# Five of the sixteen table slots read in the pause ahead of the qkv projection

## The reference, cut to what matters

```python
# first block, even layer: x += mixer; x += swiglu(rms_norm(x, e_ln_ffn), ...)   F = 2816
# first block, odd layer:
h = rms_norm(x, o_ln_mix)
q, k, v = split(h @ o_w_qkv)                 # 1024 x 3072; differential attention, 8 heads, causal
x = x + (attention(q, k, v) @ o_w_o)
x = x + moe(rms_norm(x, o_ln_ffn))           # 8 experts, top 2
# second block, layer l = 0, 1 (adaLN):
def adaln(cond, w, b):                       # w is 1024 x 6144
    m = jax.nn.silu(cond) @ w + b            # shift, scale, gate for the mixer and for the FFN
```

## Time and profile before

| | |
|---|---|
| median of 3 runs | 2750.06 us (2749.29 to 2752.14) |
| the profiled execution's own time | 2748.68 us |
| its span | 2746.9 us |
| mean granted TensorE clock | 0.992 |
| PE busy | 2642.2 us, 96% |
| DVE busy | 1903.7 us, 69% |
| ACT busy | 1400.0 us, 51% |
| DMA, mean over the span | 224 GB/s |

### The profile page before, as it was taken

The page is one execution under the profiler, slowest core; times in us unless marked ns, Lnnn a source line. Parts: engine busy times, 40 slices in busy tenths (PEclk is TensorE's granted clock), DMA queues, the critical chain, the costliest instruction groups (busy, mean ns, idle before and its releaser), DMA issues.

```text
span 2746.9 us, 46870 instructions
## 1 busy us (share of the span) xinstructions
PE 2642.2 (96%) x18575; PEld 2274.2 (83%) x18575; DVE 1903.7 (69%) x2824; ACT 1400.0 (51%) x2246; POOL 0.2 (0%) x4
## 2 busy tenths in 40 slices
PE   8899999988999999999999999999999999999998
PEld 7575997846989898989898989964899999865897
DVE  3765555746888888888888888675655655664654
ACT  2411333343777677777776777363443443253432
POOL 0000000000000000000000000000000000000000
PEclk9999999998999999999999999999999999999999
DMA  6535552584888898889898989020645442221551
GB/s 259 230 115 232 201 187 88 186 350 172 330 338 331 335 335 329 339 326 343 326 343 324 341 322 353 35 93 1 249 178 188 176 181 111 102 113 70 186 185 58
DMA packets 57000, 615.07 MB, mean 224 GB/s; under 512 B 6448, under 2 KB 6704, under 8 KB 6704
## 3 DMA queue, kind: packets, MB, share of 16 engines
q1 hardware_dynamic: 56448, 610.20, 58.8%
q10 hardware_dynamic: 432, 3.15, 0.3%
HBM read 612.28 MB, written 1.05 MB: 223 GB/s over the span
## 4 chain that ended last, share of the span: by engine, by line
PE 83%; DVE 11%; ACT 3%; issue 2%; DMA 1%; DVEq 0%; SPq 0%; ACTq 0%
PE psum L1611 8%; PE psum L1613 8%; PE psum L1612 7%; PE psum L320 6%; PE psum L322 6%; PE psum L321 6%; PE psum L510 5%; PE psum L1638 4%; PE psum L1640 4%; PE psum L1639 4%; PE psum L335 3%; PE psum L336 3%; PE psum L337 3%; PE psum L661 2%; PE psum L1996 1%
## 5 line engine op out<-in xcount | busy, mean ns | idle before, releaser
L404 DVE TENSOR_TENSOR r_high<-ring,r_high 128x1024 fp32r<-128x1024 f32 x936 | 1089.9, 1220 | 115.5 <-ACT r_high L366 114.3
L366 ACT ACTIVATE r_high<-ring 128x1024 fp32r<-128x1024 f32 x624 | 626.3, 1060 | 6.3 <-DMA ring<-stream_dram 6.3
L1611 PE MATMUL psum<-r_high 128*128 128x256 f32 x1792 | 513.8, 287 | 15.7 <-DVE r_high L1823 15.6
L1613 PE MATMUL psum<-r_high 128*128 128x256 f32 x1792 | 507.9, 283 | 0.0
L1612 PE MATMUL psum<-r_high 128*128 128x256 f32 x1792 | 507.6, 283 | 0.0
L320 PE MATMUL psum<-r_low,r_high 128*128 128x256 f32 x1408 | 399.8, 284 | 1.8 <-DVE r_high L480 1.8
L322 PE MATMUL psum<-r_low,r_high 128*128 128x256 f32 x1408 | 398.4, 283 | 0.0
L1611 PEld LDWEIGHTS psum<-r_high 128*128 128x128 f32 x1792 | 342.6, 191 | 44.3 <-issue 27.9
L1612 PEld LDWEIGHTS psum<-r_high 128*128 128x128 f32 x1792 | 342.8, 191 | 5.9 <-issue 1.7
L1613 PEld LDWEIGHTS psum<-r_high 128*128 128x128 f32 x1792 | 343.1, 191 | 0.0
L370 ACT ACTIVATE r_high<-ring 128x1024 fp32r<-128x1024 f32 x312 | 329.6, 1056 | 0.0
(11 more groups left out here) (494 smaller groups left out, 4189.7 us busy)
## 6 DMA issues: line engine op xcount, KB each, us to landing
ring<-stream_dram SPq DMA_DIRECT2D x384, 1536.0 KB, 8.1
arena<-bias_dram ACTq DMA_DIRECT2D x2, 1024.0 KB, 7.8
pack<-pack_dram SPq DMA_DIRECT2D x1, 1664.0 KB, 17.3
const<-const_dram SPq DMA_DIRECT2D x1, 1124.0 KB, 13.8
x<-x_dram SPq DMA_DIRECT2D x1, 1024.0 KB, 5.1
xc<-ctx_dram SPq DMA_DIRECT2D x1, 1024.0 KB, 24.9
arena<-band_dram ACTq DMA_DIRECT2D x1, 1024.0 KB, 5.2
out_dram<-x SPq DMA_DIRECT2D x1, 1024.0 KB, 3.9
```

The lines of the kernel that those rows point to most:

```text
L366: act.activation(w_hi[:, i % 2, part * D:part * D + D], slot_of[r][:, part * D:part * D + D], ACT.Copy)\
L404: ins = dve.tensor_tensor(lo, slot_of[r][:, o:o + D], hi.bitcast(f32), SUB)
L1611: pe.matmul(dst, xe_hi[:, k, :], hi, start=(k == 0), stop=False)
L1613: ins = pe.matmul(dst, xe_lo[:, k, :], hi, start=False, stop=(k == KD - 1))
```

## The change

The second table is read in two parts. Five of its slots (`ADA_EARLY`) stand in the ring ahead of the qkv slots: four are read right behind the FFN, in place of six of nine idle products, and the fifth behind the transposes of the norm, in place of three of five. The other eleven follow the qkv slots: eight in units 0 to 7 of the attention and three behind the loop, as before. In the ring the order is now ada1 49 to 53, qkv 54 to 61, ada1 62 to 72. In DRAM all of `ada1` stands ahead of `qkv`, and SP's loop, written out from slot 48 to 75, maps one to the other (`DRAM_AT`, `RING_AT`). `ada_z_dve(dve, 1)` moves from behind the qkv columns to just ahead of `ffn_dve`, and its array and that of the copied rows move into constants no longer used (`g2`, `w2a2`). The first part is copied out of PSUM by ACT between `x_hi` and the sine, and DVE adds the second part from PSUM behind the scaling by the root. The remaining idle products write bank 5, since bank 7 now holds the table.

```diff
 STREAM = [
...
-    ("qkv", QKV // COLS), ("ada1", ADA_SLOTS), ("o_out", 3),
+    ("ada1", ADA_SLOTS), ("qkv", QKV // COLS), ("o_out", 3),
...
+ADA_EARLY = 5
+RING_AT = {_name: FIRST[_name] for _name in FIRST}
+RING_AT["qkv"] = FIRST["ada1"] + ADA_EARLY
+RING_AT["ada1_rest"] = RING_AT["qkv"] + QKV // COLS
+DRAM_AT = [*range(FIRST["ada1"], FIRST["ada1"] + ADA_EARLY), *range(FIRST["qkv"], FIRST["o_out"]),
+           *range(FIRST["ada1"] + ADA_EARLY, FIRST["qkv"])]
...
-        cond_z = [ar(o, KD * 62, "p (k n) -> p k n", k=KD) for o in (29200, 25600)]
-        ada_rows = [ar(o, COLS) for o in (28816, 27648)]
+        cond_z = [t.rearrange("p (k n) -> p k n", k=KD) for t in (ar(29200, KD * 62), mat("g2")[:, 0:KD * 62])]
+        ada_rows = [ar(28816, COLS), mat("w2a2")[:, 0:COLS]]
...
         def ada_slot(l, s):
+            if l:
+                return RING_AT["ada1"] + s if s < ADA_EARLY else RING_AT["ada1_rest"] + s - ADA_EARLY
...
-            starts = (0,) if l else (0, ADA_SPLIT)
+            starts = (0, ADA_EARLY if l else ADA_SPLIT)
...
-        def ada_rows_dve(dve):
+        def ada_rows_dve(dve, l):
 
-            slot_used(dve, ada_slot(0, ADA_SLOTS - 1))
-            dve.wait_ge(sem("ada_rows"), 1)
-            step(dve, dve.tensor_tensor(ada_rows[0], ada_rows[0], psum[:, 6, 0:COLS], ADD), "ada_rows")
+            slot_used(dve, ada_slot(l, ADA_SLOTS - 1))
+            dve.wait_ge(sem("ada_rows"), 2 * l + 1)
+            step(dve, dve.tensor_tensor(ada_rows[l], ada_rows[l], psum[:, 6 + l, 0:COLS], ADD), "ada_rows")
...
             diff_cols_dve(dve)
-            ada_z_dve(dve, 1)
...
                 S(dve.tensor_tensor(v, v, rstd[:, 8 * j:8 * j + 8].unsqueeze(2).to_broadcast([P, 8, P]), MUL), "df_on")
+            ada_rows_dve(dve, 1)
...
                 act.activation(x_hi[:, half, :], hT[:, half, 0:T], ACT.Copy).then_inc(sem("px_hi"), 1)
+            ada_rows_act(act, 1, ADA_EARLY)
             diff_cols_act(act)
...
             root_act(act, 16)
-            ada_rows_act(act, 1)
...
-                if n < ADA_1:
-                    ada_pe(pe, 1, n, n + 1)
+                if ADA_EARLY + n < ADA_1:
+                    ada_pe(pe, 1, ADA_EARLY + n, ADA_EARLY + n + 1)
...
-            with sp.Fori(1, min(G_MOE, g_end)) as g:
+            n0, n1 = FIRST["ada1"], FIRST["o_out"]
+            with sp.Fori(1, n0 // RING) as g:
                 for r in range(RING):
                     sp.wait_ge(w_used[r], g)
                     sp.dma_start(slot_of[r], stream_in[g * RING + r]).then_inc(w_ready[r], 16)
+            for n in range(n0 // RING * RING, G_MOE * RING):
+                sp.wait_ge(w_used[n % RING], n // RING)
+                sp.dma_start(slot_of[n % RING], stream_in[DRAM_AT[n - n0] if n0 <= n < n1 else n])\
+                  .then_inc(w_ready[n % RING], 16)
...
             ffn_pe(pe, 0, "e_ffn")
-            idle_pe(pe, 9)
+            ada_pe(pe, 1, 0, ADA_EARLY - 1)
+            idle_pe(pe, 3, 5)
             norm_pe(pe, 2)
-            idle_pe(pe, 5)
+            ada_pe(pe, 1, ADA_EARLY - 1, ADA_EARLY)
+            idle_pe(pe, 2, 5)
             diff_pe(pe)
...
             ada_mods_dve(dve, 0)
+            ada_z_dve(dve, 1)
             ffn_dve(dve, 0, "e_ffn")
```

More of the change, by code:

```diff
@@ L571, in ada_slot @@
         def ada_slot(l, s):
+            if l:
+                return RING_AT["ada1"] + s if s < ADA_EARLY else RING_AT["ada1_rest"] + s - ADA_EARLY
             late = s - (ADA_SLOTS - ADA_LATE)
-            return FIRST["ada0_late"] + late if l == 0 and late >= 0 else FIRST[f"ada{l}"] + s
+            return FIRST["ada0_late"] + late if late >= 0 else FIRST["ada0"] + s
         def ada_pe(pe, l, s0, s1):
@@ L590, in ada_pe, with ada_rows_act @@
                 ins.then_inc(w_used[n % RING], 1)
-        def ada_rows_act(act, l, slots=ADA_SLOTS):
+        def ada_rows_act(act, l, slots):
             slot_used(act, ada_slot(l, slots - 1))
             act.activation(ada_rows[l], psum[:, 6 + l, 0:COLS], ACT.Copy).then_inc(sem("ada_rows"), 1)
-        def ada_rows_dve(dve):
-            slot_used(dve, ada_slot(0, ADA_SLOTS - 1))
-            dve.wait_ge(sem("ada_rows"), 1)
-            step(dve, dve.tensor_tensor(ada_rows[0], ada_rows[0], psum[:, 6, 0:COLS], ADD), "ada_rows")
+        def ada_rows_dve(dve, l):
+            slot_used(dve, ada_slot(l, ADA_SLOTS - 1))
+            dve.wait_ge(sem("ada_rows"), 2 * l + 1)
+            step(dve, dve.tensor_tensor(ada_rows[l], ada_rows[l], psum[:, 6 + l, 0:COLS], ADD), "ada_rows")
         def ada_tr_pe(pe, l):
-            pe.wait_ge(sem("ada_rows"), l + 2)
+            pe.wait_ge(sem("ada_rows"), 2 * l + 2)
             for c in range(COLS // P):
@@ L1203, in split_proj @@
             ph, pl = [parts(o, n * KD // 2 * COLS, "p (b n) -> p b n", b=n) for o in (hi, lo)]
-            return {"tag": tag, "n0": FIRST[name], "widths": widths, "tiles": tiles, "n": n, "hi": ph, "lo": pl, "x": x,
+            return {"tag": tag, "n0": RING_AT[name], "widths": widths, "tiles": tiles, "n": n, "hi": ph, "lo": pl, "x": x,
                     "x_ready": x_ready, "turn": turn,
@@ L3035, in _ @@
             rwkv_out_dve(dve)
-            ffn_norm_dve(dve, 1, 0, "e_ffn", x_tm, lambda c: vec("e_ln_ffn", c), None, lambda: ada_rows_dve(dve), True,
+            ffn_norm_dve(dve, 1, 0, "e_ffn", x_tm, lambda c: vec("e_ln_ffn", c), None, lambda: ada_rows_dve(dve, 0), True,
                          ctx_rstd)
             ada_mods_dve(dve, 0)
+            ada_z_dve(dve, 1)
             ffn_dve(dve, 0, "e_ffn")
```

## The result

The changed kernel takes 2763.3 us (median of 5 runs, 2759.1 to 2764.4) beside 2750.6 for the kernel before; the ratio is 1.0033 with a 95% interval of 1.0021 to 1.0045. Repeated, beside runs of the kernel before on the same chip, it is 1.0030 (1.0020 to 1.0041), 2762.5 against 2753.8. By the ratios that is 8 to 9 us slower, where 6.5 was forecast. The first pair of medians alone lies 12.7 us apart; the kernel before has medians of 2750.6, 2752.8, 2753.8 and 2756.0 in the four sets of runs of this study, so one pair of medians is good to a few us only. The profiled execution took 2759.09 us, 10.4 us more than that of before.

A forecast was written before the change was run, and what follows sets the result against it. PE, busy 96% of the span, was taken to bound the kernel. Pause +13.0, ada_z +0.7 and loop -7.2 gave +6.5 us on 2750.06, so 2756.6; own range 2755.4 to 2757.9, stated range 2753.2 to 2762.0.

The forecast's parts named there:

- the pause: Between the even block's FFN and the qkv projection: ACT's root, and with it the projection, 13.0 us later.
- the loop: Attention units 8 to 12 lose their reads and go at 2.32 us each: -7.2 us, bounds 5.3 to 8.8.
- the rival on the clock: Low clock at the projection's start and in the attention's second half: +8.3 to +13.3 us, 2758.4 to 2763.4; chance 0.15.
- a low stretch in the projection or the loop: Sign of being wrong: PE's clock falls in the qkv projection or attention units; 1.00 was expected from the projection on.
- 12.0 and 14.0 for the root: Bounds on how much later ACT's norm root runs ahead of the qkv projection, in us, around the forecast 13.0.
- the ring's gate: After the FFN, a slot's transfer is issued only when the slot four places ahead has been used; slots 54, 55 wait.
- the quick one: Of two earlier transfer bursts, the one landing 6.2, 8.5 and 10.9 us after issue; slot 55 at 15.0 us.
- the middle: Slot 55 landing 16.0 us after PE's first read behind the FFN, taken between 15.0 and 17.0.
- The estimate from the Trainium skill: HBM to SBUF near 358 GB/s, 4.4 us a slot: third transfer some 2 us later, sum +8.6.
- ada_z: Clearing and copy for the second table, moved ahead of `ffn_dve`, delay the first FFN product: +0.7 us, bound 0.
- The rival that took the chain's DMA entries at their word: Attention loop bound by stream transfers: five fewer save 18.5 us, sum -4.8, 2745.3; chance 0.05.
- The one in which reads are free: Reads in the attention loop cost nothing, so removing them gains nothing there: +13.7 us, 2763.8; chance 0.05.

The follow-up runs named there:

- Root first: Changed kernel with ACT taking the norm's root ahead of the first qkv weight pieces, DVE's order changed to match, transfers and reads kept: 2748.8 us, ratio 0.9990 to before.
- the ordered queues with products: Changed kernel with ACT and DVE queues in order of readiness, `ada_z` in the FFN's last turns, extra idle products: 2744.7 us, ratio 0.9968 to before; again 2744.0, 0.9962.
- the twelve slots: Kernel before with four of the second table's sixteen slots neither transferred nor read, so units 9 to 12 hold no read: 2748.9 us, ratio 0.9984 to before.
- the filled units: Changed kernel with two idle products in each of units 8 to 12 in place of the reads that left, no transfer: 2765.9 us, ratio 1.0044 to before.
- the ordered queues on the kernel before: Kernel before, all sixteen reads in the attention, ACT taking root, x_hi, then pieces, DVE scaling, x_lo, then low parts: 2752.0 us, ratio 0.9991 to before.
- the bare version: Changed kernel with five early reads, queues in order of readiness and `ada_z` moved, but no extra idle products: 2748.2 us, ratio 0.9974 to before.
- the warm pause: Changed kernel with 17 idle products in place of three behind the four early reads, so PE works through the wait for the root: ratio 1.0032 to before.

## Why the prediction was right, point by point

The two large terms, the pause and the loop, came out as forecast. Their sum, +6.5 us with its own range up to 2757.9, was too low: the +9.1 of the first ratio lies inside the stated range but in the band of the rival on the clock (+8.3 to +13.3), which had a chance of 0.15. The first median, 2763.3, lies 1.3 us over the upper end of the range, 2762.0. The prediction also named a low stretch in the projection or the loop as a sign that it is wrong, and one stood in the loop. In the profiled executions the 10.4 us are the forecast's 6.5, less 0.5 in the pause and 0.3 in the units, plus 3.1 in the attention and 3.5 behind it, both at stretches of low clock, less 2.0 because the part up to the end of the FFN was quicker in this execution. That last part is luck. Two small slips stand in the prediction's sums: with 12.0 and 14.0 for the root its own range comes to 2755.6 to 2757.6, and the lower end of the clock's rival, 1.8 us over the forecast, has no row.

*The pause.* The mechanism was right in each link: the ring's gate, the burst, the pieces, the root behind them. Forecast +13.0, measured 30.6 - 18.1 = +12.5 in the profile, +13.0 in the repeat. The burst was the quick one (10.9 for the third; 11.0 to 11.7 in the other traces with five early reads), so the middle was 1 us too late; by the quick one alone the forecast would have been 12.0. The projection started at 479.0, ahead of the 480.4 to 482.4 that the prediction named, because PE's reads began at 448.5 and not at 449.6 and a little later. Root first, with the same transfers, removes 11 us of it, and the scan over two, four and five reads costs nothing at two and 9 us at four, as the ring has it. This cause is shown.

*The transfers.* The third transfer landed 10.9 us after its issue, as in the earlier trace rows; the landings of the burst are 3.7 us apart. The estimate from the Trainium skill, DMA: Bandwidth & Descriptors, section "Where 436 GB/s comes from", 4.4 us a slot, would have had it 2 us later. The trace does not agree with it for this core.

*ada_z.* In the changed trace the clearing starts at 258.11 and x_lo at 258.82, 0.7 us, as forecast. The first FFN product came at 261.2, not at 263.2; it lies between 261.2 and 266.7 in the traces here, with other stretches of low clock in it, so its time does not show this term. PE's wait ahead of it does (timeline of PE):

```profile
261.24 0.39 PE L326 MATMUL psum<-r_low,r_high 128*128 128x256 f32 x1 [1.04 <-DVE r_high L486]
```

It waited 1.04 us, where it waited 0.19 before. In both traces of the ordered queues with products, in which `ada_z` has moved into the FFN's last turns, the wait is 0.19 again.

*The loop.* Forecast -7.2 for units 8 to 12; measured 11.29 - 18.83 = -7.5. The rival that took the chain's DMA entries at their word is out by this and by the twelve slots; the filled units leave the transfers at most 3.5 of the 7.5 us. The one in which reads are free is out as well.

*The clock.* This is the term that was mis-sized: the forecast had it at nothing and kept it as a rival. Loop and tail together went from 61.9 to 57.5 (57.9 in the repeat), 4.4 us, of 7.5 that the units gained: half a clock at the start of the attention (2.2 us) and behind its last scores (0.9) gave 3 us back. The rival had the mechanism and one place nearly right, the second half of the attention; at the start of the projection nothing was lost in the profiled execution, and 1.5 us in the repeat.

The stretch at the start of the scores is not the price of the reads that left. It stands in ten of the thirteen traces, the ordered queues on the kernel before among them, which keep all their reads; root first and the bare version, with five early reads, do not have it. PE had been as busy ahead of it in the changed kernel (3.57 us of 7.0, from 546.0) as in the kernel before, where the clock stayed at 1.00 (3.75 of 7.0, from 534.5). Why it falls in one execution and not in another is not shown. The tail is 15.8 to 17.5 us in the six traces where it holds a low stretch and 14.8 or 14.9 in the seven where it holds none. All six have at least four units fewer with a read and no product in their place. Of the seven, four have reads or products in those units (before, ordered queues on before, two early reads with a read up to unit 10, filled units), two have the products behind the scores, and one, with four early reads, has neither. So in the tail the reads of the loop were most likely cover for the clock as well as work; the trace with four early reads is the exception. Against the bare version the extra products brought 2 to 4 us, with intervals that overlap, and they were added at two places and not tried one by one. The prediction's reason against this rival, units 13 to 15 at a clock of 1.00 in the earlier trace rows, came from a stretch that reads stood directly ahead of and behind.

After the wait the sixteen transposes took 3.67 us, against 1.97 in the earlier trace rows; the projection in the profiled execution, which came after 7.4 us of work, ran at a clock of 1.00, and in the repeat a low stretch fell into it. The Trainium skill, TensorE: Matmul & The Clock Gate, section "HAM oscillation — how this bites in real kernels", has the burst after a wait for a DMA start cold. By these rows that holds for the transposes and not for the projection of the profiled execution.

*Behind the attention.* The changed kernel was another 3.5 us longer there in both its traces: 1.5 to 1.8 us up to the first expert product, 1.8 in the rest. It is no fixed cost of the change: with the same code behind the attention the warm pause has 1014.6 in the rest and the filled units 30.3 and 1014.8. The rest goes closely with the low clock inside it over all thirteen traces, from 1014.2 us with 11.0 at 1.2 GHz (before) through 1015.5 with 12.0 (root first) and 1016.0 with 13.0 (changed) to 1017.3 with 14.5 (four early reads). The way to the experts goes with it less closely: 28.4 us with 3.4 at 1.2 GHz, 30.2 to 30.4 with 10.2, 31.6 to 32.0 with 13.7, 33.3 with 17.1, but 31.7 with 10.2 where four slots are read early. The two traces with the products behind the scores are the ends of this list, from the same kernel.

*What stays open.* Why the clock falls longer there after one attention than after another, and at the start of the scores in most executions and not in all, was not settled.

## What to carry to other kernels

When a transfer is moved behind new work, ask who stands behind its reader on the same engine: here a 0.2 us root came 12 us later for weights that it does not need. Put each engine's queue in the order in which its inputs become ready, and prefetch only as deep as the ring allows (two early reads cost the pause nothing, four cost it 9 us; three were not tried). And work that fills a gap may hold the clock of the stage that follows: count that when it is taken out.

## What the runs showed of the hardware

- A burst of 1536 KB transfers issued 1.3 us apart landed after 6.1, 8.5, 10.9 and 13.3 us, within 0.1 us of the burst of the earlier trace rows, the landings 3.7 us apart; in the other traces with five early reads the third took 11.0 to 11.7.
- The table load for the root (1.28 us) ran at 443.99, ahead of ACT's wait for DVE, once nothing stood between it and the FFN's last activation (root first); behind the pieces it was on the path, at 466.38.
- TensorE fell to 1.2 GHz while it still had work: in the changed kernel at the start of the scores (6.70 of 6.70 us busy, clock 0.54) and behind the last scores (5.66 of 8.40 us busy, clock 0.82). Behind the last scores of the ordered queues, with two more products, it kept 1.00 (13.07 of 15.00 us busy).
- 3.4 us at 1.2 GHz inside the projection cost 1.5 us (67.7 against 66.1 or 66.2).
